# Bank-by-bank waits for the residual adds in the MLP loop of a two-block network on one core

## What is computed

```python
def first_block(...):
        ...
        x = x + merged @ w_out[l]
        xn = rms_norm(x, ffn_norm_g[l])
        gate, up = jnp.split(xn @ w_gate_up[l], 2, axis=-1)
        x = x + (jax.nn.silu(gate) * up) @ w_down[l]
    return rms_norm(x, final_norm_g)

def second_block(...):
        ...
        h = rmsnorm(x, w_norm_ffn[l])
        u = causal_dwconv(h @ w_ffn_up[l], w_ffn_conv[l])
        gate, val = jnp.split(u, 2, axis=-1)
        x = x + (jax.nn.silu(gate) * val) @ w_ffn_down[l]
    return rmsnorm(x, w_norm_final)
```

## Time and profile before

| | |
|---|---|
| median of 3 runs | 2984.84 us |
| lowest and highest | 2983.16 and 2987.18 us |
| the profiled execution | 2986.03 us |
| its span, from the first instruction to the last | 2984.3 us |
| granted TensorE clock, mean of the span | 0.967 of full speed |
| PE busy | 2730.1 us (91%) |
| DVE busy | 1296.2 us (43%) |
| POOL busy | 1139.2 us (38%) |
| ACT busy | 659.6 us (22%) |

### The profile page before, as it was taken

How to read it: one execution, slowest core, us unless ns; L and a number is a source line. 1 busy time by engine, 2 the same in 40 slices (tenths; PEclk the granted TensorE clock), 3 DMA queues, 4 the chain that set the end, 5 groups by cost and what they waited for, 6 DMA issues and landing times. The chain is left out here.

```text
span 2984.3 us, 35045 instructions
## 1 busy us (share of the span) xinstructions
PE 2730.1 (91%) x12987; PEld 2179.2 (73%) x12987; DVE 1296.2 (43%) x1819; ACT 659.6 (22%) x1173; POOL 1139.2 (38%) x901
## 2 busy tenths in 40 slices
PE   4999888999999999969999488869899999999996
PEld 2887456888888888858888377864588888888885
DVE  4032542323433333360530366657324555566546
ACT  3010651200000000050330333335222211111113
POOL 2442125244444444423554143300523444554541
PEclk9999998999999999989999689989999999999998
DMA  3111003111111111121111000000311111111111
GB/s 101 47 50 46 29 15 113 29 49 45 51 46 49 46 49 46 54 81 43 49 49 31 0 1 1 1 1 1 124 32 36 47 45 49 46 49 49 46 56 64
DMA packets 91204, 131.53 MB, mean 44 GB/s; under 512 B 9461, under 2 KB 57824, under 8 KB 91112
## 3 DMA queue, kind: packets, MB, share of 16 engines
q1 hardware_dynamic: 88808, 121.88, 13.5%
q10 hardware_dynamic: 2304, 8.39, 0.7%
HBM read 121.82 MB, written 8.42 MB: 44 GB/s over the span
## 5 line engine op out<-in xcount | busy, mean ns | idle before, releaser
L123 POOL TENSOR_TENSOR w_hi<-w_raw,zero 128x512 fp32r<-128x512 f32 x352 | 407.5, 1158 | 1226.5 <-PE bank L980 502.4
L978 PE MATMUL bank<-xt_hi,w_hi 128*128 128x512 f32 x1312 | 513.0, 391 | 15.8 <-DVE x_sb L1254 14.1
L125 POOL TENSOR_TENSOR w_lo<-w_raw,w_hi 128x512 fp32r<-128x512 f32 x352 | 510.9, 1452 | 27.6
L979 PE MATMUL bank<-xt_lo,w_hi 128*128 128x512 f32 x1312 | 510.9, 389 | 0.0
L980 PE MATMUL bank<-xt_hi,w_lo 128*128 128x512 f32 x1312 | 510.5, 389 | 0.0
L1254 DVE TENSOR_TENSOR x_sb<-bank,x_sb 128x512 f32<-128x512 f32 x320 | 221.3, 691 | 213.9 <-PE bank L1014 213.9
L978 PEld LDWEIGHTS bank<-xt_hi,w_hi 128*128 128x128 f32 x1312 | 246.2, 188 | 75.1 <-DVE x_sb L1254 21.7
L980 PEld LDWEIGHTS bank<-xt_hi,w_lo 128*128 128x128 f32 x1312 | 246.3, 188 | 51.6
L979 PEld LDWEIGHTS bank<-xt_lo,w_hi 128*128 128x128 f32 x1312 | 246.3, 188 | 50.6
L177 PE MATMUL bank<-xt_hi,w_hi 128*128 128x512 f32 x512 | 199.3, 389 | 0.0
L177 PE MATMUL bank<-xt_lo,w_hi 128*128 128x512 f32 x512 | 199.2, 389 | 0.0
(11 more groups left out here) (410 smaller groups left out, 4580.9 us busy)
## 6 DMA issues: line engine op xcount, KB each, us to landing
w_raw<-in_w_gate_up_dram SPq DMA_DIRECT2D x88, 256.0 KB, 3.1
w_raw<-in_w_ffn_up_dram SPq DMA_DIRECT2D x88, 256.0 KB, 3.1
w_raw<-in_w_mix_in_dram SPq DMA_DIRECT2D x48, 256.0 KB, 2.7
w_raw<-in_w_down_dram SPq DMA_DIRECT2D x44, 256.0 KB, 2.6
w_raw<-in_w_ffn_down_dram SPq DMA_DIRECT2D x44, 256.0 KB, 2.6
w_raw<-in_w_in_dram SPq DMA_DIRECT2D x40, 256.0 KB, 2.7
x_sb<-in_x_dram SPq DMA_DIRECT2D x8, 512.0 KB, 6.9
gate_rows<-gate_sums SPq DMA_DIRECT2D x8, 512.0 KB, 4.9
```

Of the source, the lines that this page charges most:

```text
L123: pool.tensor_tensor(m.w_hi[:, u, :], m.w_raw[:, u, :], zeros, ALU.add).then_inc(m.hi_done, 1)
L125: pool.tensor_tensor(m.w_lo[:, u, :], m.w_raw[:, u, :], m.w_hi[:, u, :].bitcast(F32), ALU.subtract).then_inc(m.split, 1)
L978: pe.matmul(m.psum[b][:, :], u_hi[:, col], m.xt_hi[:, k, tok], start=k == 0, stop=False)
L979: pe.matmul(m.psum[b][:, :], u_hi[:, col], m.xt_lo[:, k, tok], start=False, stop=False)
```

## The change

The counter `dn_ev` starts at `NB` = 8 in place of 1, and each bank of the up product waits for 16 `i` + `b` + 1 in place of 16 `i` + 1. After the turn before, the counter stands at 8 + 16 `i`; the add of bank `b` in its second column half is the one that brings it to 16 `i` + `b` + 1. So a bank waits for the last add that reads it, not for those of the banks behind it. All other waits on `dn_ev` are rewritten for the new start value and wait for the same adds as before.

```diff
--- before.py
+++ after.py
@@ -1028,30 +1028,30 @@
-                            pe.wait_ge(dn_ev, 16 * i + t + 2)
+                            pe.wait_ge(dn_ev, 16 * i + NB + t + 1)
...
             with pe.Fori(0, FI - 1) as i:
                 def wait_bank(b):
                     pe.wait_ge(ev_d if b % 2 else ev_a, 4 * i + b // 2 + 1)
-                    pe.wait_ge(dn_ev, 16 * i + 1)
+                    pe.wait_ge(dn_ev, 16 * i + b + 1)
                 up(loop + 12 * i, wait_bank)
                 down(loop + GU + 12 * i, i)
             pe.wait_ge(m.split, loop + 12 * (FI - 1) + 4)
-            pe.wait_ge(dn_ev, 16 * (FI - 1) + 1)
+            pe.wait_ge(dn_ev, 16 * (FI - 1) + NB)
...
-                        pe.wait_ge(dn_ev, 16 * (FI - 1) + 1 + 2 * (t - 4) + nh + 1)
+                        pe.wait_ge(dn_ev, 16 * (FI - 1) + NB + 2 * (t - 4) + nh + 1)
...
-                        pe.wait_ge(dn_ev, 16 * FI + 1)
+                        pe.wait_ge(dn_ev, 16 * FI + NB)
...
-                    act.wait_ge(dn_ev, 16 * (FI - 1) + 1 + 2 * t + 2)
+                    act.wait_ge(dn_ev, 16 * (FI - 1) + NB + 2 * t + 2)
...
-            dve.memset(raw[:, :, 0:PAD], 0.0).then_inc(dn_ev, 1)
-            dve.wait_ge(dn_ev, 1)
+            dve.memset(raw[:, :, 0:PAD], 0.0).then_inc(dn_ev, NB)
+            dve.wait_ge(dn_ev, NB)
```

## The result

| | before | changed |
|---|---|---|
| median | 2985.20 us (6 runs) | 2964.23 us (6 runs) |
| lowest and highest | 2983.16 and 2989.06 us | 2961.24 and 2965.69 us |
| the profiled execution | 2986.03 us | 2965.69 us |
| its span | 2984.3 us | 2963.9 us |

The ratio is 0.9928 with a 95% interval of 0.9915 to 0.9940: the changed kernel is 0.72% faster. Forecast were 2964.7 us, between 2960.7 and 2970.1.

The account below looks back on a forecast made before the run. PE, busy 91% of the span, was taken to bound the kernel. Two crossings between turns at 1.10 us and sixteen at 1.12 give 20.1 us: 2984.84 - 20.1 = 2964.7 us, range 2960.7 to 2970.1.

Parts of the forecast that it names:

- The sum: PE's crossings from one turn to the next, two at 1.10 us and sixteen at 1.12 us, win 20.1 us together.
- The list: PE's waits in the profile: the up product's first matmul line waits for DVE's residual add, 14.1 us in 18 waits.
- the slow steps behind it: PE's slower matmul steps right behind each crossing between turns, 0.16 to 0.18 us, forecast to go with the standing still.
- What is late next: In the loops, the third and fourth weight slices keep 9 and 11 us of cover; the gain passes through to the end.
- the long waits behind the loops: PE's single waits at the last down products, 7.4 and 17.7 us, forecast to stay as long as they are.
- The register operations: Seven more in each turn on PE's sequencer, forecast to cost zero, hidden by its lead; upper end 17 us.
- Slow steps that stay: Rival at the crossings between turns: only the standing still goes, 17.0 us, giving 2967.8 us; chance 0.10.
- The return in place of the wait: Rival at the loop's return: fetching instructions outlasts the 3.5 us lead and PE stands; at worst 2984.8 us; chance 0.05.
- instruction packets inside the loops: Sign in the changed trace's loops that would prove the forecast wrong; none was seen from 680 to 1280 us before.
- A fall of the clock without pauses: Rival in the loops: PE without pauses drops to the lower clock, a step costing about 0.2 us more; chance 0.02.
- The count: Rival at the banks' waits: a bank's value is reached only by a later add, the wait stays, 2984.8 us; chance 0.02.
- The ends of the range: 2960.7 us if both last down products went at full clock; 2970.1 us for slow steps staying plus 2.3 us of scatter.

## Why the prediction was right

**The sum.** 66.38 or 66.40 us less 65.28 was to be won at each of eighteen crossings. Every one of the changed kernel's turns takes 65.28 us. Eighteen times that difference is 20.1 us, and the two spans differ by 20.4. The rest is not the change's: 0.2 us of it lie ahead of the first loop, which starts at 610.07 us in place of 610.24, and 0.1 behind the last. And no turn hides a loss: the two loops, from the first matmul to one step behind the last, are ten times 65.28 us long, PE is busy throughout, and the clock reads 1.00 (us, PE busy, granted clock, DMA share):

```profile
610.07:1262.87 652.80, 652.80 (x2881) 1.00 0.17 49
2262.76:2915.56 652.80, 652.80 (x2881) 1.00 0.16 48
```

**Reading steps, not the list of waits.** The list had 14.1 us. The 6 us more are the part of each stop that the modelled end of a matmul covers (0.94 less 0.78 us, 2.9 us in eighteen stops), and the slow steps behind it (3.1 us). That both would go was the point on which the forecast differed from the plain reading, and both went.

**What is late next.** Nothing, as forecast: POOL takes the third slice at 674.91 with the same 6.00 us of idle time before it, the clock reads 1.00 in both loops, and the long waits behind the loops are the same, so the gain went through to the end.

**The register operations.** Zero, as forecast. They take the place of seven separate waits, as was thought possible, but that isn't what the zero needs: 48 more of them cost the array nothing either. The price of 0.12 us each, which only set a bound, was too high; it is 0.093.

**The rivals.** Slow steps that stay: out, in all kernels in which PE doesn't stand. The return in place of the wait: out for this kernel, whose branch takes 0.231 us at the same crossing and whose loop brings in no code behind its first turn. The forecast had said that instruction packets inside the loops would prove it wrong. Two of q8 do stand in the first turn of the changed kernel, between 610 and 672 us, on its first way through the body, and two in the same place of the kernel before:

```profile
q8 instruction: 2, 0.03, 0.2%
```

The next comes at 1271 us, behind the loop. None lies at a return, the only place where one could have cost PE what the forecast feared.

A fall of the clock without pauses: out; both loops read 1.00 over 652.8 us on end. The count: out. The ends of the range were not needed: in the changed trace, too, both last down products begin with steps of 0.43 us.

The Trainium skill, page Runtime: NRT & Kernel Launch, section Instruction fetch mechanics, which the forecast had weighed against the change, says that a taken branch out of the present window fetches its target before anything goes on. For the body of five turns the trace agrees: 3.31 us of branch, and instruction packets. For the body of one turn it does not: 576 matmuls and weight loads lie between branch and target, more than two pages of 256 instructions, and the branch takes 0.235 us, with no packet of that queue behind the first turn. The same section gives PE's store as 2048 instructions, which lies between one turn and five, and by that the two cases are told apart.

## What to carry to other kernels

A wait that asks for the last of a row of events, where the first user needs only the first of them, can cost the engine the tail of that row at every round; ask of each such wait which event its own instruction needs, and look at the first two users above all, since here they were worth the whole gain, as was asking for the last event but one. Take what it costs from start-to-start steps and from the length of a whole round against a round without the wait, not from the list of waits alone. And once the wait is loose, spend the slack: here it let another engine's work move forward, which before would have been paid back at each round.

## What the runs showed beyond expectation

- The PE sequencer runs 3.5 to 4.0 us ahead of the array in these loops, and this lead hid a branch of 3.31 us completely; with a lead of 1.7 us at the branch (931.7 against 933.41) one of 3.65 us cost 2.35 us of standing. A loop of one turn (576 matmuls and weight loads) returns in 0.235 us.
- A matmul that waits for a semaphore holds the sequencer too: in the run in which bank 0 alone waits for the adds, register operations behind it came only with its release, 4.5 us later.
- A pause of 2.35 us of PE was followed by eight steps of 0.41 to 0.43 us (the stretch from 937.4 to 940.9 us reads a granted clock of 0.60), and that turn took 1.7 us longer; behind the pause of 2.56 us in the second stage it was 1.8 us. The eighteen pauses of 0.94 us in the kernel before left the clock at 1.00.
- Register operations with fulfilled waits cost the PE sequencer 0.093 us each, and the array nothing for 48 of them spread over eight banks.
